# The downward product of an MLP by seven block products in place of eight

## What is computed

```python
def sq_relu_mlp(h, w_up, w_down):                 # w_up (1024, 4096), w_down (4096, 1024)
    return jnp.square(jax.nn.relu(h @ w_up)) @ w_down
...
h2 = modulate(rmsnorm(x, norm2_g[l]), sh2, sc2)
x = x + g2 * sq_relu_mlp(h2, w_up[l], w_down[l])
```

## Time and profile before

| | us |
|---|---|
| runs, median of 3 | 3135.5 (3135.24 to 3142.22) |
| profiled execution, its time | 3143.2 |
| its span, first to last instruction | 3141.4 |
| TensorE busy (matmuls) | 2971.8 (95%) |
| VectorE busy | 1496.1 (48%) |
| GpSimd busy | 1044.8 (33%) |
| ScalarE busy | 921.0 (29%) |
| mean granted TensorE clock | 0.985 of full speed |

### The profile page before, as it was taken

The page is one execution under the profiler, slowest core; times in us unless marked ns, Lnnn a source line. Parts: engine busy times, 40 slices in busy tenths (PEclk is TensorE's granted clock), DMA queues, the critical chain, the costliest instruction groups (busy, mean ns, idle before and its releaser), DMA issues.

```text
span 3141.4 us, 37191 instructions
## 1 busy us (share of the span) xinstructions
PE 2971.8 (95%) x14854; PEld 2456.3 (78%) x14854; DVE 1496.1 (48%) x2276; ACT 921.0 (29%) x1604; POOL 1044.8 (33%) x458
## 2 busy tenths in 40 slices
PE   7999999999999999999999999998999999999996
PEld 3786778888787888888887877786887877777785
DVE  5833138887624314132224453546146566654545
ACT  5122326664113101010101112303145455543302
POOL 1333241001585444344444443242421212112242
PEclk9999999999999999999999999998999999999998
DMA  5534573221533111111111211111341121211112
GB/s 236 184 128 149 193 242 86 71 71 52 183 114 108 47 47 47 53 47 47 47 53 40 67 54 48 41 47 28 102 128 49 53 60 54 54 48 48 34 47 87
DMA packets 118659, 258.84 MB, mean 82 GB/s; under 512 B 47292, under 2 KB 69340, under 8 KB 114288
## 3 DMA queue, kind: packets, MB, share of 16 engines
q1 hardware_dynamic: 118512, 256.81, 25.3%
HBM read 212.30 MB, written 45.97 MB: 82 GB/s over the span
## 4 chain that ended last, share of the span: by engine, by line
PE 73%; DVE 16%; ACT 5%; issue 2%; DMA 2%; SPq 1%; POOL 1%; ACTq 0%; DVEq 0%; POOLq 0%
PE ps L423 22%; PE ps L425 21%; PE ps L424 21%; ACT tmp L1735 3%; DVE tmp L2459 2%; PE ps L1265 2%; PE ps L1632 2%; DVE acc L2263 2%; DVE tmp L2897 2%; DVE Ea L2236 2%; PE ps L1618 1%; PE ps L1253 1%; DMA raw<-in_w 1%; DVE Z L2239 1%; DVE mx L2681 1%
## 5 line engine op out<-in xcount | busy, mean ns | idle before, releaser
L830 POOL TENSOR_TENSOR whi<-raw,onesf 128x1024 fp32r<-128x1024 f32 x191 | 368.7, 1930 | 1949.1 <-PE ps L425 1875.1
L423 PE MATMUL ps<-Hb_hi,whi 128*128 128x512 f32 x1424 | 574.4, 403 | 17.4 <-DVE Y L2654 5.9
L425 PE MATMUL ps<-Hb_hi,wlo 128*128 128x512 f32 x1424 | 556.7, 391 | 0.0
L424 PE MATMUL ps<-Hb_lo,whi 128*128 128x512 f32 x1424 | 556.3, 391 | 0.0
L832 POOL TENSOR_TENSOR wlo<-raw,whi 128x1024 fp32r<-128x1024 f32 x191 | 514.7, 2695 | 15.0
L423 PEld LDWEIGHTS ps<-Hb_hi,whi 128*128 128x128 f32 x1424 | 268.8, 189 | 69.7 <-issue 14.1
L425 PEld LDWEIGHTS ps<-Hb_hi,wlo 128*128 128x128 f32 x1424 | 268.0, 188 | 58.1
L424 PEld LDWEIGHTS ps<-Hb_lo,whi 128*128 128x128 f32 x1424 | 269.0, 189 | 48.0
L1735 ACT ACTIVATE tmp<-tmp,mx 128x1280 f32<-128x1280 f32 (+2 forms) x192 | 187.2, 975 | 105.8 <-DVE mx L2897 90.5
L1735 ACT ACTIVATE tmp<-ps 64x256 f32<-64x256 f32 (+2 forms) x97 | 57.8, 596 | 545.5 <-PE ps L425 472.3
L423 PE MATMUL ps<-Uhi,whi 128*128 128x512 f32 x512 | 199.2, 389 | 0.0
(11 more groups left out here) (455 smaller groups left out, 5813.2 us busy)
## 6 DMA issues: line engine op xcount, KB each, us to landing
raw<-in_w SPq DMA_DIRECT2D x201, 512.0 KB, 3.3
adas<-in_ada SPq DMA_DIRECT2D x16, 1024.0 KB, 4.9
raw<-in_w SPq DMA_DIRECT2D x44, 256.0 KB, 3.9
adaE<-in_ada SPq DMA_DIRECT2D x4, 2048.0 KB, 23.0
gate_d<-gst SPq DMA_DIRECT2D x16, 512.0 KB, 2.7
v_d<-VS SPq DMA_DIRECT2D x2, 4096.0 KB, 14.2
ncB<-cum_d SPq DMA_DIRECT2D x16, 512.0 KB, 3.6
Vx<-v_d SPq DMA_DIRECT2D x16, 512.0 KB, 4.3
```

What stands on the lines that cost most here:

```text
L423: nc.tensor.matmul(o, wh, xh, start=start, stop=False)
L424: nc.tensor.matmul(o, wh, xl, start=False, stop=False)
L425: return nc.tensor.matmul(o, wl, xh, start=False, stop=stop)
L830: nc.gpsimd.tensor_tensor(whi[b][:, 0:w], raw[b][:, 0:w], onesf[:, 0:1].to_broadcast([P, w]), ALU.mult).then_inc(S("split_hi"), 1)
```

## The change

The downward product is made by Strassen's scheme. There are now eight parts of 512 inner features. In each, the 512 inner features, the 1024 outputs and the 1024 tokens are halved, so the product is one of 2 x 2 blocks (weight blocks 512 outputs x 256 inner, operand blocks 256 inner x 512 tokens). Instead of eight block products there are seven, of sums of blocks; each product is added to one or two of the four blocks of the output, with a sign.

- TensorE: per part 4 upward tiles of 48 matmuls as before, and 7 products of 24 matmuls (4 output tiles x 2 steps x 3). Each product has two halves `h`, and each half fills a "unit" of two PSUM banks. There are now four units, all 8 banks (`unit`, `unit_free`). Product x waits for its weights (`split`) and for the lower halves of its operands (`u_lo` at `LOW_BEFORE[x]`).
- VectorE: squares are gone from it (ScalarE makes them). It makes the operand sums `Usum` (0, 3, 4, 5, 6) for each of the two 128-feature steps `k`, and the lower halves of the seven operands; after each half product it adds 2 x (1 or 2) pieces of 128 x 512 into `X1` straight from PSUM, with `modx` or its negative `negmod`. Some of the updates stand between the operand work of the second step (`BESIDE`).
- ScalarE: relu, square, the upper halves of the operands, and the upper halves `whi` of the seven weight sums (`l_hi`).
- GpSimd: splits the 4 upward panels of a part, adds or subtracts the weight blocks (`l_sum`, 5 a part, into `raw`) and makes the lower halves `wlo` of the 7 (`l_low`).
- SP: loads four raw weight blocks a part (`Lraw`), in pieces of 256 columns, besides the upward panels.
- The hardware loops of the stage are gone; the code of all parts is written out. The rest of the diff renames semaphores (`sq_acc` to `sums_made`, `rows_full` to `half_full`, `ada_early` to `EARLY`) and renumbers panels and tiles. The panels of the stages behind are the same.

```diff
+MLP_PARTS, UPS, UNITS = 8, 4, 18
+UP_ORDER = (0, 2, 1, 3)
+SUMMED = ((2, 0, "subtract"), (2, 3, "add"), (0, 1, "add"), (1, 3, "subtract"), (0, 3, "add"))
+TARGETS = (((1, 1, 1),), ((1, 0, 1), (1, 1, -1)), ((0, 0, -1), (0, 1, 1)), ((0, 0, 1),), ((0, 0, 1), (1, 1, 1)), ((0, 1, 1), (1, 1, 1)), ((0, 0, 1), (1, 0, 1)))
+LOW_BEFORE = (8, 8, 9, 10, 11, 12, 12)
...
+                for p in range(MLP_PARTS):
+                    for j in (2, 3):
+                        split_up(p, j)
+                    gp.wait_ge(S("l_loaded"), 16 + 64 * (p + 1))
+                    l_sum(p, 0)
+                    l_sum(p, 1)
+                    for x in range(7):
+                        if x < 5:
+                            gp.wait_ge(S("l_sum"), 16 + 5 * p + x + 1)
+                        l_low(p, x)
+                        if x < 3:
+                            l_sum(p, x + 2)
+                    for j in range(2):
+                        split_up(p + 1, j)
...
-                with pe.Fori(0, 4) as i:
-                    for t in range(8):
-                        tile("mlp", 16, i, t, 16, t, Hb[0], Hb[1], ready=(lambda k: pe.wait_ge(S("ap_lo"), 16 + k + 1)) if t == 0 else None)
-                    for t in range(8):
-                        tile("mlp", 16, i, 8 + t, 16, 8 + t, Uhi, Ulo,
-                             ready=(lambda k: pe.wait_ge(S("u_lo"), 8 * i + k + 1)) if t == 0 else None)
+                def product(p, x):
+                    n = part_panel(p, UPS + x)
+                    pe.wait_ge(S("split"), n + 1)
+                    pe.wait_ge(S("u_lo"), 12 * p + LOW_BEFORE[x])
+                    for h in range(2):
+                        u = UNITS * p + UPS + 2 * x + h
+                        unit_free(pe, u - 4)
+                        for c in range(2):
+                            o = unit(u)[0][:, HALF * c:HALF * c + HALF]
+                            for k in range(2):
+                                w = slice(256 * (2 * h + c) + P * k, 256 * (2 * h + c) + P * k + P)
+                                last = mm3(o, whi[n % 2][:, w], wlo[n % 2][:, w], Uhi[:, x, k, :], Ulo[:, x, k, :], k == 0, k == 1)
+                        if h == 0:
+                            last.then_inc(S("half_full"), 1)
+                    done(last)
...
+                def up(p, j):
+                    n, u = part_panel(p, j), UNITS * p + j
+                    g, free, before = unit(u)
+                    b = tmp[j % 2][:, 0:T]
+                    act.wait_ge(S("panel_done"), n + 1)
+                    if p or j >= 2:
+                        act.wait_ge(S("u_lo"), 12 * p + 6 * (j // 2))
+                    copy(b, g, free, ACT.Relu)
+                    act.wait_ge(free, before + u // 4 + 1)
+                    copy(b, b, S("u_sq"), ACT.Square)
...
+                for p in range(MLP_PARTS):
+                    for k in range(2):
+                        up(p, 2 * k)
+                        if k:
+                            l_hi(p, 0)
+                        operand_hi(p, k, 1, 2 * k + 1, tmp[0][:, 0:HALF])
+                        operand_hi(p, k, 0, 1)
+                        if k:
+                            l_hi(p, 1)
+                        up(p, 2 * k + 1)
+                        operand_hi(p, k, 2, 2 * k + 2, tmp[1][:, HALF:T])
+                        operand_hi(p, k, 3, 2)
+                        if k:
+                            l_hi(p, 2)
+                        operand_hi(p, k, 4, 3)
+                        if k:
+                            l_hi(p, 3)
+                        act.wait_ge(S("sums_made"), 16 + 10 * p + 5 * k + 5)
+                        copy(Uhi[:, 5:7, k, :], Usum[:, 5:7, k, :], S("u_hi"))
+                    for x in range(4, 7):
+                        l_hi(p, x)
...
+                def second_tile(p, k, beside):
+                    a, b = tmp[0], tmp[1]
+                    dve.wait_ge(S("u_sq"), 4 * p + 2 * k + 2)
+                    operand_sum(3, k, b[:, left], b[:, right], ALU.add)
+                    operand_lo(p, k, 2, 3, b[:, right])
+                    beside(0)
+                    operand_lo(p, k, 3, 4)
+                    beside(1)
+                    operand_sum(4, k, a[:, left], b[:, right], ALU.add)
+                    beside(2)
+                    operand_lo(p, k, 4, 5)
+                    beside(3)
+                    operand_sum(5, k, a[:, right], b[:, right], ALU.subtract)
+                    operand_sum(6, k, b[:, left], a[:, left], ALU.subtract)
+                    beside(4)
+                    dve.wait_ge(S("u_hi"), 12 * p + 6 * k + 6)
+                    sub(Ulo[:, 5:7, k, :], Usum[:, 5:7, k, :], Uhi[:, 5:7, k, :], S("u_lo"))
...
+                BESIDE = (((0, 0), (0, 1)), ((1, 0),), ((1, 1),), ((2, 0),), ((2, 1),))
+                for p in range(MLP_PARTS):
+                    first_tile(p, 0)
+                    second_tile(p, 0, lambda m: None)
+                    first_tile(p, 1)
+                    second_tile(p, 1, lambda m: [update(p, *xh) for xh in BESIDE[m]])
+                    for x in range(3, 7):
+                        for h in range(2):
+                            update(p, x, h)
```

More of the change, by code:

```diff
@@ L820, in twice @@
                 two = [P0["gates"] + 2, P0["gates"] + 3] + list(range(P0["merge"], P0["wout"])) + [P0["fox"] + kq_panel(h) for h in range(FOX)]
-                return sum(1 for m in two if m <= n and (m - n) % 2 == 0)
+                return sum(1 for m in two if m <= n and (m - n) % 2 == 0) - (28 if n >= P0["pool"] else 0)
             def split(n, i=0, per=0, w=PW):
@@ L1996, in act_program @@
             if on("mlp"):
[L1997 to L2005, removed]
@@ new lines, in operand_hi, with l_hi @@
+                def operand_hi(p, k, x, after, of=None):
+                    if of is None:
+                        act.wait_ge(S("sums_made"), 16 + 10 * p + 5 * k + after)
+                        of = Usum[:, x, k, :]
+                    else:
+                        act.wait_ge(S("u_sq"), 4 * p + after)
+                    copy(Uhi[:, x, k, :], of, S("u_hi"))
+                def l_hi(p, x):
+                    n = part_panel(p, UPS + x)
+                    act.wait_ge(S("panel_done"), n - 1)
+                    if x < 5:
+                        act.wait_ge(S("l_sum"), 16 + 5 * p + x + 1)
+                    copy(whi[n % 2][:, :], raw[x % 2][:, :] if x < 5 else Lraw[0 if x == 5 else 3], S("split_hi"))
@@ L2598, in dve_program @@
             if on("mlp"):
[L2599 to L2610, removed]
+                nc.vector.tensor_scalar(negmod, modx[:, 40:48], -1.0, None, ALU.mult).then_inc(S("mods"), 1)
@@ new lines, in dve_program, with operand_sum, operand_lo, first_tile @@
+                dve.wait_ge(S("mods"), 19)
+                left, right = slice(0, HALF), slice(HALF, T)
+                def operand_sum(x, k, a, b, op):
+                    tt(Usum[:, x, k, :], a, b, op, S("sums_made"))
+                def operand_lo(p, k, x, after, of=None):
+                    dve.wait_ge(S("u_hi"), 12 * p + 6 * k + after)
+                    sub(Ulo[:, x, k, :], Usum[:, x, k, :] if of is None else of, Uhi[:, x, k, :], S("u_lo"))
+                def first_tile(p, k):
+                    dve.wait_ge(S("u_sq"), 4 * p + 2 * k + 1)
+                    operand_sum(0, k, tmp[0][:, left], tmp[0][:, right], ALU.add)
+                    operand_lo(p, k, 1, 1, tmp[0][:, left])
+                    operand_lo(p, k, 0, 2)
@@ new lines, in update @@
+                def update(p, x, h):
+                    u = UNITS * p + UPS + 2 * x + h
+                    g, free, _ = unit(u)
+                    if h == 0:
+                        dve.wait_ge(S("half_full"), 7 + 7 * p + x + 1)
+                    else:
+                        dve.wait_ge(S("panel_done"), part_panel(p, UPS + x) + 1)
+                    if p or x:
+                        unit_free(dve, u - 2 if x else UNITS * p - 2 + h)
+                    for c in range(2):
+                        for i, t, sign in TARGETS[x]:
+                            m = 4 * i + 2 * h + c
+                            x_ = X1[:, m, HALF * t:HALF * t + HALF]
+                            last = nc.vector.scalar_tensor_tensor(x_, g[:, HALF * c:HALF * c + HALF], (modx[:, 40 + m:41 + m] if sign > 0 else negmod[:, m:m + 1]), x_, ALU.mult, ALU.add)
+                    last.then_inc(free, 1)
```

132 lines of the change are left out of this document (102 added, 30 removed).

## The result

| | before | changed |
|---|---|---|
| runs, median of 4 | 3137.9 us (3135.2 to 3142.2) | 3194.6 us (3192.0 to 3200.2) |
| profiled execution: span | 3141.4 | 3190.2 |
| mean granted TensorE clock | 0.985 | 0.975 |

The ratio is 1.018 (95% interval 1.016 to 1.020): slower by 57 us or 1.8%, where +20 was forecast and 3172 us was the upper end of the range.

A forecast was written before the change was run, and what follows sets the result against it. TensorE's issue was taken to bound the MLP stage. Stops of 63 us, minus 43.5 saved, plus 0.7 at the stage's end gave +20: 3163 us for the profiled execution, 3155.5 for the median; range 3128 to 3172.

The forecast's parts named there:

- Gaps of some us will not change its clock: TensorE in the MLP: waits of a few us were claimed to leave its clock unchanged, so no cost was counted.
- signs of being wrong: Stated refutations: parts 81.6 us apart, X1 updates also held by GpSimd, or operands in time because the alternation fell out differently.
- Product 0: First downward product of each part: TensorE stops 3.7 us for lower halves of operands delayed by VectorE and GpSimd alternating.
- Products 3 and 4: Downward products of each part: TensorE stops 0.8 and 3.4 us for weights delayed behind operand sums and X1 updates.
- The end of the stage: MLP's end: first `Hb_lo` waits about 5.5 us with no second wait; 0 to 3 us more, taken as 0.7.
- The saving: Downward product: 24 matmuls fewer in each of 8 parts, 43.5 us saved on TensorE if nothing new stops it.
- Priority for VectorE or GpSimd: Two rivals on who goes first where both ask: VectorE, 3124 to 3147 us, 17%; GpSimd, 3176 us, 4%.
- Sharing: Rival: VectorE and GpSimd slow each other instead of excluding, 512-column operations take twice 0.69 us; 3104 to 3121 us, 12%.
- the order and the alternation: Operand and weight work: VectorE and GpSimd exclude each other and alternate, so its order makes TensorE stop 7.9 us a part.

The follow-up runs named there:

- the three kernels with stops added: The kernel before, with TensorE waits added in or behind the MLP's upward product, aimed at 3, 6 and 1 us: 3158.8, 3174.7 and 3189.6 us.
- the reordered kernel: The changed kernel with only the order of work on GpSimd, ScalarE and VectorE altered to remove all three stops of a part: 3100.8 us, ratio to before 0.988.
- the weight sums of 16 columns: The changed kernel with GpSimd's five weight sums of a part cut from 1024 to 16 columns, left incomplete: 3154.6 us.
- the kernel without product 0's stop: The changed kernel with GpSimd's weight sum 0 ahead of panel 3's split and ScalarE's upper half of operand 1 ahead of product 0's weight copy: 3162.7 us.
- only the stops of product 0 left: The changed kernel with VectorE's and ScalarE's work reordered to remove only the stops at products 3 and 4: 3140.8 us, ratio to before 1.001.

## Why the prediction failed

**The term that was put at nothing: the clock.** "Gaps of some us will not change its clock" was read off one place, where 3.27 and 1.61 us of waiting left matmuls at 0.40. It was luck of that execution: in the three kernels with stops added, the same wait of 3.27 us at the same place is followed by twelve slow matmuls in the one with stops of 3 us, by six in that of 6 us and by none in that of 1 us. And the trace of before held the contrary at the start of the stage, behind a wait of 2.56 us, in a stretch that the prediction doesn't use (same columns as above):

```profile
983.50:987.00 3.50, 3.50 (x10) 2.73 (x9) 3.44 (x3) 2.50 (x3) 3.42 (x2) 0.52 0.38 139
```

The changed kernel has some 140 slow matmuls in its parts, 0.43 - 0.23 = 0.20 us each: 28 us. No rival in the prediction and none of its signs of being wrong spoke of the clock, so the range couldn't hold it.

**The stops were right.** Product 0: 3.7 forecast, 3.57 in the rows, and 3.73 from slot to slot, a slot being the 0.23 us till the next matmul could start (1213.64 + 0.23 to 1217.60). Products 3 and 4: 0.8 and 3.4 forecast, 0.74 and 3.18. Their sum is 60.0 us. Each also costs 0.16 us, by which a matmul's end trails its slot, and 0.11, by which the second matmul behind a stop starts later; the first was in the forecast, the second not. 60.0 + 24 x 0.27 = 66.5 against 63.

**The end of the stage** was put at 0.7 more. One wait of 5.70 us came for the first `Hb_lo` (5.5 were forecast), where 4.9 stood, but ten slow matmuls behind it make another 2: +2.8.

```profile
1738.38 0.77 PE L448 MATMUL ps<-Hb_hi,whi 128*128 128x512 f32 x1 [5.70 <-DVE Hb_lo L2391]
```

The sum by these rows: -43.5 + 66.5 + 28 + 2.8 = +53.8. From the first matmul of the stage to the end of the span the two traces differ by 2212.3 - 2158.8 = 53.5 us. So the account closes, and of the 34 us between forecast and trace 28 are the clock, 3.5 the stops and 2 the end. The whole spans differ by only 49, since the changed trace reaches the stage 4.7 us earlier (977.9 against 982.65). So do the traces of the three kernels with stops added, whose code ahead of the stage is that of before (976.7 to 978.2), so this isn't the change's doing. The medians differ by 57, where executions of one kernel differ by 7 to 8 us among themselves.

**The saving** was right: 448 `Uhi` matmuls of each kind, and without stops 43 us less stage (980.98 to 1639.9 in the reordered kernel, against 982.65 to 1684.9).

**The rivals.** Priority for VectorE or GpSimd didn't occur; the rows of the alternation above settle it. Sharing is excluded by the same rows, and by the weight sums of 16 columns. The Trainium skill (SBUF — State Buffer, section SBUF: two separate sides) calls the pair of ports that VectorE and GpSimd share an exclusive lock, held for the whole instruction. The rows agree: a held operation ends its bare duration less some 0.14 us after the other's end (0.54 and 0.55 against 0.69, 2.26 against 2.39), and no two overlap.

**What a stop is worth** is thus what the prediction lacked; its mechanism, the order and the alternation, was right. Had each of the 24 stops been priced at its length and 0.27, and each of the 16 long ones at 28 / 16 = 1.75 more for the clock, the forecast would have been -43.5 + 66.5 + 28 + 0.7 = +52.

**What stays open.** Why equal stops cost between 0 and 14 slow matmuls from part to part: the runs show the spread, not what sets it. Why only one of the five stops of 1.57 to 1.77 us in the kernel without product 0's stop was followed by slow matmuls is open too, and so are 2 of the 6 us that the reordered kernel is short of its sum.

## What to carry over

A stop of TensorE of some 3 us costs about half as much again, in slow matmuls behind it: price it so, and look for half clock behind every wait of the trace before, not behind one. When work moves to VectorE and GpSimd at once, count not their busy shares but the operations with two SBUF inputs that meet GpSimd's, one by one; if the sum of work fits, the order can be mended without changing any of it, here by having ScalarE and GpSimd make what TensorE needs next ahead of what it needs later. A stop of 1.3 us costs its length and 0.27, so where idle time can't be avoided, short stops are cheaper: 42 us of it in stops of 1.3 cost 54 us, 14 us in stops of 3.4 cost 23.

## What was not expected of the hardware

- TensorE at 1.2 GHz behind stops of 3.2 to 3.6 us: 6 to 14 matmuls at 0.43 us instead of 0.23, in all 16 cases of the changed kernel; in 6 of 8 with only the stops of product 0 left, in 7 of 8 stops of 3.50 us with product 0's taken away.
- No such stretch behind any of 32 stops of 1.3 us, 42 us of idle time in all; but seven or eight slow matmuls behind the wait of 2.4 to 2.6 us at the start of the stage, in nine of nine traces.
- VectorE and GpSimd alternated without exception wherever both had operations with SBUF inputs queued, each waiting for one of the other's: 2.88 us for a lower half of 0.69, time after time. In the stage of the changed kernel there is no place where one of them got two in a row while the other waited.
